# Two decoder layers on one core: activation tiles by ScalarE's DMA queue, two raw weight buffers, other token chunks, norm pieces and weight sums on VectorE

## The reference

```python
def rms_norm(x, g, eps=RMS_EPS):
    xf = x.astype(jnp.float32)
    y = xf * lax.rsqrt(jnp.mean(xf * xf, axis=-1, keepdims=True) + eps)
    return (y * g.astype(jnp.float32)).astype(x.dtype)

def swiglu(xn, w_gate, w_up, w_down):
    h = jax.nn.silu(jnp.einsum('bsd,df->bsf', xn, w_gate)) * jnp.einsum('bsd,df->bsf', xn, w_up)
    return jnp.einsum('bsf,fd->bsd', h, w_down)
...
        hp = hp + swiglu(rms_norm(hp, ln_ffn[layer]), w_gate[layer], w_up[layer], w_down[layer])
        hs = hs + swiglu(rms_norm(hs, ln_ffn[layer]), w_gate[layer], w_up[layer], w_down[layer])
```

## Time and profile before

| | us |
|---|---|
| median of three runs | 2750.6 |
| the profiled execution's own time | 2745.67 |
| its span, first to last instruction | 2743.8 |
| TensorE busy / VectorE / ScalarE / GpSimd | 2385.8 / 1658.9 / 972.0 / 850.5 |
| mean granted TensorE clock | 0.951 of full speed |

### The profile page before, as it was taken

The page is one execution under the profiler, slowest core; times in us unless marked ns, Lnnn a source line. Parts: engine busy times, 40 slices in busy tenths (PEclk is TensorE's granted clock), DMA queues, the critical chain, the costliest instruction groups (busy, mean ns, idle before and its releaser), DMA issues. The chain is left out here.

```text
span 2743.8 us, 47200 instructions
## 1 busy us (share of the span) xinstructions
PE 2385.8 (87%) x17889; PEld 2183.8 (80%) x17889; DVE 1658.9 (60%) x3570; ACT 972.0 (35%) x2144; POOL 850.5 (31%) x863
## 2 busy tenths in 40 slices
PE   8999998888899799999987887786999999878876
PEld 6788766555699699999987886786999899878876
DVE  4312166556755866767665665488767676656655
ACT  5211134455742433333332112454333333322123
POOL 0010100354321344343432225532343434322243
PEclk9999999999999899999998998898999999988988
DMA  4331499655620242434374443202433333744433
GB/s 155 106 108 44 156 388 405 221 168 168 207 69 16 97 161 104 157 108 147 118 297 172 153 161 106 77 21 97 155 110 141 124 128 136 283 187 153 153 115 108
DMA packets 178850, 410.13 MB, mean 149 GB/s; under 512 B 9683, under 2 KB 115492, under 8 KB 170187
## 3 DMA queue, kind: packets, MB, share of 16 engines
q1 hardware_dynamic: 172835, 359.70, 36.4%
q0 software_dynamic: 5808, 47.64, 5.0%
HBM read 302.52 MB, written 138.31 MB: 161 GB/s over the span
## 5 line engine op out<-in xcount | busy, mean ns | idle before, releaser
L2490 PE MATMUL ps<-xnr,wc 128*128 128x272 f32 x6336 | 854.3, 295 | 40.7 <-issue 15.6
L2490 PEld LDWEIGHTS ps<-xnr,wc 128*128 128x128 f32 x6336 | 835.6, 194 | 44.0 <-issue 42.0
L2490 PE MATMUL ps<-x2b,wc 128*128 128x272 f32 x2376 | 349.2, 302 | 141.9 <-DVE x L2059 97.1
L2490 PEld LDWEIGHTS ps<-x2b,wc 128*128 128x128 f32 x2376 | 324.9, 199 | 157.2 <-DVE x L2059 81.8
L2490 PE MATMUL ps<-x2a,wc 128*128 128x272 f32 x2376 | 335.8, 298 | 78.4 <-DVE ot L2003 45.8
L2490 PEld LDWEIGHTS ps<-x2a,wc 128*128 128x128 f32 x2376 | 319.4, 196 | 86.3 <-DVE wc L1958 48.4
L1302 POOL TENSOR_TENSOR wsum<-wr 128x512 f32<-128x512 f32 (+2 forms) x90 | 96.9, 1077 | 796.9 <-DMA wr<-w_down 389.0
L1958 DVE TENSOR_TENSOR wc<-wr,wc 128x512 fp32r<-128x512 f32 (+2 forms) x270 | 199.0, 737 | 213.4 <-ACT wc L1526 213.4
L1526 ACT ACTIVATE wc<-wr 128x512 fp32r<-128x512 f32 (+2 forms) x270 | 142.2, 527 | 406.9 <-DMA wr<-w_down 223.3
L2231 PE MATMUL ps<-wp,xn 128*128 128x512 f32 (+1 forms) x1080 | 245.4, 389 | 0.0
L2231 PEld LDWEIGHTS ps<-wp,xn 128*128 128x128 f32 (+1 forms) x1080 | 196.3, 182 | 48.9
(11 more groups left out here) (277 smaller groups left out, 3300.9 us busy)
## 6 DMA issues: line engine op xcount, KB each, us to landing
hidden<-stg SPq DMA_DIRECT2D x40, 1904.0 KB, 8.6
xnr<-hidden SPq DMA_DIRECT2D x40, 1088.0 KB, 10.3
wr<-w_up SPq DMA_DIRECT2D x22, 1024.0 KB, 10.2
wr<-w_gate SPq DMA_DIRECT2D x20, 1024.0 KB, 5.3
kraw<-cache_win_k_a SPq DMA_DIRECT2D x8, 2048.0 KB, 14.8
vraw<-cache_win_v_a SPq DMA_DIRECT2D x8, 2048.0 KB, 11.6
kraw<-cache_k_b SPq DMA_DIRECT2D x64, 256.0 KB, 5.8
vraw<-cache_v_b SPq DMA_DIRECT2D x64, 256.0 KB, 11.1
```

Source lines behind the costliest of these rows:

```text
L2490: r = mm(out, wc[:, q, a, kt * P:(kt + 1) * P], slot(moving_at(u, kt), q, b_), start=(q < 4 and kt == 0 and i == 0), stop=(kt == n - 1 and ...
```

## The change

- The hidden stores, the slot loads and the reload of x are issued by ScalarE, at places written into its stream, and no longer by SyncE. Slot loads of the second piece (n = 4 to 7) are moved to units 45 and 46.
- SyncE issues only the weights. The load of set w waits for the last set that used the same part of `wr` (`set_before`). `wr` grows from 2048 to 3072 columns: sets of depth 2 and 3 alternate between two places, sets of gate and up (depth 4) still have one. In layer 1 set 0 has a tile of its own, `wr0`. The copy of x to DRAM is issued ahead of set 1.
- The two sums in `wsum` for the sets of gate and up are made by VectorE, at the start of the unit before the set; GpSimd still makes the other two, and all four in the down pieces.
- The token chunks are 384, 288, 416 ahead of layer 0's FFN and 384, 256, 448 ahead of layer 1's (with 3, 2 and 4 row tiles).
- All norm differences go to VectorE, as single instructions over four tiles (128 x 1088), and so do the high and low parts of the normalised tiles. The quarters of tp 1 come later in unit 0, between its parts.
- The low parts of both hidden tiles of a block are made in the next block's first unit (gate tp 0), no longer half of them in the unit up tp 1. The stores follow in that unit's part 5 and the next unit's part 2.

```diff
-CH = ((0, 384), (384, 384), (768, 320))
+CH = {1: ((0, 384), (384, 288), (672, 416)), 3: ((0, 384), (384, 256), (640, 448))}
...
+        def set_place(w):
+
+            n = 512 * set_depth(w)
+            at_ = n * (w % 2) if n < 2048 else 0
+            return at_, at_ + n
+
+        def set_before(w):
+
+            a0, a1 = set_place(w)
+            return max(v for v in range(1, w) if set_place(v)[0] < a1 and a0 < set_place(v)[1])
...
                 if w == 1:
-                    sp.wait_ge(norm_pieces, 16 * norm_block(layer, 1) + 1)
+                    sp.wait_ge(norm_pieces, 16 * norm_block(layer, 1) + 16)
                 else:
-                    sp.wait_ge(set_lo, PARTS * set_number(layer, w))
+                    sp.wait_ge(set_lo, PARTS * (set_number(layer, set_before(w)) + 1))
...
             def ffn_sp(layer):
 
                 set_load(layer, 0)
-                set_load(layer, 1)
-                sp.wait_ge(norm_pieces, 16 * norm_block(layer, 1) + 16)
+                sp.wait_ge(group_added, ADD_PER * (layer + 1))
                 sp.dma_start(x_kept[:], x[:]).then_inc(x_stored, 16)
-                for u in range(UNIT_L):
-                    kind, b, _, tp = ffn_at(u)
-                    w = set_at(u)
-                    for n in range(SLOTS):
-                        if n not in KEPT and slot_free(n) == u - 1:
-                            slot_load(layer, n)
-                    if u == set_begin(w) and 1 <= w < SETS - 1:
-                        set_load(layer, w + 1)
-                    if 2 <= u - 1 < UNIT_A - 4 and ffn_at(u - 1)[0] == "up":
-                        hidden_store(layer, *ffn_at(u - 1)[1::2])
+                for w in range(1, SETS):
+                    if w == SETS - 2:
                         sp.wait_ge(part_done, done(layer, UNIT_Z + 3, PARTS - 1))
+                        sp.wait_ge(blocks_added, 24 * layer + 12)
...
+                    set_load(layer, w)
...
+            def transfers(layer, u, q):
+
+                b, r = divmod(u - 4, 4)
+                if 0 <= b < PAIRS - 1 and (r, q) in ((0, 5), (1, 2)):
+                    hidden_store(layer, b, r)
+                if (u, q) == (UNIT_A - 3, 6):
+                    x_load(layer, 0)
+                if (u, q) == (UNIT_A - 2, 2):
+                    x_load(layer, 1)
+
+            def slot_loads(layer, u):
+
+                for n in range(SLOTS):
+                    if n not in KEPT and u == (UNIT_A + 1 + n // 6 if 4 <= n < 8 else slot_free(n) + 1):
+                        slot_load(layer, n)
...
+                        if u == set_end(w) and w + 1 < UNIT_A // 2 and q == 0:
+                            set_sum(layer, w + 1)
                         if u == set_end(w) and w < SETS - 1 and q:
                             set_low(layer, w + 1, q - 1)
-                        if 0 < u <= UNIT_A and ffn_at(u - 1)[0] == "up" and q >= 3:
+                        if u in (UNIT_A - 1, UNIT_A) and q >= 3:
                             for i in ((0, 1), (2, 3), (4, 5), (6,))[q - 3]:
                                 hidden_low(layer, u - 1, i)
+                        elif 4 <= u < UNIT_A and u % 4 == 0:
+                            for i in ((0, 1, 2), (3, 4), (5, 6), (0, 1), (2, 3), (4, 5), (6,))[q]:
+                                hidden_low(layer, u - 2 if q < 3 else u - 1, i)
```

More of the change, by code:

```diff
@@ L562, in norm_block, with norm_at @@
             return 2 * layer + tp
+        NORM_PIECES = (((0, 0), (1, 0), (0, 1), (1, 1)), ((0, 0), (0, 1), (1, 1), (1, 0)))
+        NORM_SUMS = (V1, V2, V3, V4), (V1, V2, V4, V3)
+        NORM_HI = (V11, V21, V22, V2, V1, V3, V4), (V11, V2, V1, V3, V21, V22, V4)
+        NORM_LO = V11, V2, V1, V3, V21, V22, V4
+        def norm_at(order, n, tp, what):
+            return len(order[tp]) * n + order[tp].index(what) + 1
         def chunk_sum_bank(c):
@@ L1525, in set_high @@
                     act.wait_ge(set_sums, 4 * set_number(layer, w) + {2: 1, 1: 2, 3: 3, 5: 4}[q])
[L1526 removed]
+                act.activation(set_cols(w, wc[:, q, 0]), set_source(layer, w, q), ACT.Copy).then_inc(set_hi, 1)
             def norm_high(layer, tp, q):
                 n = norm_block(layer, tp)
[L1531 to L1539 removed]
+                place = {V11: (0, 0), V21: (1, 0), V22: (1, 1)}.get(q)
+                if place:
+                    act.wait_ge(norm_pieces, 4 * norm_at(NORM_PIECES, n, tp, place))
+                else:
+                    act.wait_ge(norm_sums, norm_at(NORM_SUMS, n, tp, q))
+                act.activation(normed(tp, q, 0), normed_plain(tp, q), ACT.Copy).then_inc(norm_hi, 1)
             def hidden_high(layer, u, q):
@@ L1943, in norm_low @@
             def norm_low(layer, tp, q):
                 n = norm_block(layer, tp)
-                place = (V11, V21, V22, V2, V1, V3, V4).index(q)
-                dve.wait_ge(norm_first, 8 * n + (8 if q in (V3, V22) else 4))
-                if q in (V2, V4):
-                    dve.wait_ge(norm_second, 8 * n + 8)
-                for kt in range(4):
-                    phys = kt + 4 * tp
-                    dve.wait_ge(norm_hi, 28 * n + 4 * place + kt + 1)
-                    tt(slot(phys, q, 1), slot_plain(phys, q), slot(phys, q, 0).bitcast(F32), ALU.subtract).then_inc(norm_lo, 1)
+                reader = {V11: V1, V2: V4, V1: V2, V3: V3, V21: V4, V22: V3, V4: V4}[q]
@@ new lines, in norm_low, with set_sum @@
+                dve.wait_ge(norm_sums, norm_at(NORM_SUMS, n, tp, reader))
+                dve.wait_ge(norm_hi, norm_at(NORM_HI, n, tp, q))
+                tt(normed(tp, q, 1), normed_plain(tp, q), normed(tp, q, 0).bitcast(F32), ALU.subtract).then_inc(norm_lo, 1)
+            def set_sum(layer, w):
+                n = set_number(layer, w)
+                dve.wait_ge(set_loaded[w % 2], set_loads(layer, w))
+                dve.wait_ge(set_lo, PARTS * n)
+                tt(set_cols(w, wsum[:, 0]), raw_quarter(layer, w, 0, 1), raw_quarter(layer, w, 1, 1), ALU.add).then_inc(set_sums, 1)
+                dve.wait_ge(set_sums, 4 * n + 1)
+                tt(set_cols(w, wsum[:, 1]), set_cols(w, wsum[:, 0]), raw_quarter(layer, w, 0, 0), ALU.subtract).then_inc(set_sums, 1)
@@ L2042, in down_out @@
                     if p:
-                        tt(kept, src, kept, ALU.add).then_inc(parts_dve, 1)
+                        tt(both, src, both, ALU.add).then_inc(parts_dve, 1)
                     return
@@ L2097, in ffn_dve @@
                     if u == 0:
-                        for v in (V1, V3, V21, V22, V4):
+                        norm_sum(layer, 1, V4)
+                        norm_low(layer, 1, V2)
+                        norm_low(layer, 1, V1)
+                        norm_sum(layer, 1, V3)
+                        for v in NORM_LO[3:]:
                             norm_low(layer, 1, v)
```

241 lines of the change are left out of this document (124 added, 117 removed).

## The result

The changed kernel takes 2514.3 us in the median of 4 runs (2510.5 to 2519.6), against 2750.4 for the kernel before (4 runs): ratio 0.914, 95% interval 0.912 to 0.916. The forecast was 2502, with 2465 to 2565 as its range. The profiled execution took 2515.3 us with a span of 2513.5, so 230.3 us of span are gone.

The account below looks back on a forecast made before the run. TensorE loses some 180 us per layer waiting on late weights or at lower clock afterwards. Savings 2 x (37 + 3.7 + 41.5 + 35 + 7) = 248.4 us give 2497.3 profiled, so 2502 forecast; range 2465 to 2565.

Parts of the forecast that it names:

- Gate and up: From unit 2: three stalls per block go, 37 us less per layer, 3.7 of 40.7 staying as slips; bounds 25 to 40.7.
- VectorE becomes the bound: Rival in gate and up: VectorE overloaded in up tp 1, load late again, 2.7 us per block, 2556 us; chance 0.13.
- Units 44 and 45: Weights no longer behind six slot loads, last hidden tile's order unchanged: 3.7 us less per layer, bounds -4 and 10.
- 4.62 and 1.8 less 1.8 and 1.5: Units 44 to 46: unit 45's stall and slow clock go; a ScalarE issue stall of 1.8 and slow clock of 1.5 come.
- Down pieces: From unit 46: weights load one set earlier, in a queue without slot loads; 41.5 us less per layer, bounds 30 and 44.
- the 3.3 us that I left: Down pieces: loss expected to remain of 44.8 us per layer, at the step from depth 2 to 3.
- its slot is freed too late in both kernels: Down pieces, step from depth 2 to 3: reason given, beside places one behind the other, for the 3.3 us left.
- The first rival: Down pieces: weights served in issue order behind slot loads, 4 us late plus 1.6 slow clock, six times; 2536 us; chance 0.10.
- the loop that I followed: Last piece: VectorE's last result through GpSimd's add, sums, high and low parts, back to last result; 8.6 us per period.
- The rival of 11.5 us: Last piece stays in its chain: GpSimd's adds between its sums, period 11.5 us, 2 x 20 less won, 2542; chance 0.12.
- Units 0 and 1: VectorE has fewer, larger instructions and less contention with GpSimd: 7 us less per layer, bounds -5 and 15.
- 2 us earlier: Units 0 and 1: VectorE's work from the reciprocal starts 2 us earlier, results of parts 1 and 2 going ahead of quarters.

Follow-up runs that it names:

- The kernel with x behind the weights: Against the changed kernel: SyncE reloads x behind the first two down sets, ScalarE's root behind norm pieces, last norm sum earlier; 2502.9 us, ratio 0.909.
- one place: Against the changed kernel: down weight sets back to one raw place, each load waiting for the copies of the set before; 2639.1 us profiled.
- lows spread: Against the changed kernel: hidden low parts back to seven behind each up unit instead of fourteen in gate tp 0; 2536.9 us profiled.

## Why the prediction was right, step by step

**Gate and up, 37 forecast, 38.3 and 39.5 measured.** The mechanism holds: the low parts moved, the load lands in 5.3, and the three stalls are gone. With the low parts spread again the second stall alone came back, and only with SyncE's queue and GpSimd's sums on top the old 483, which is the order of causes that the prediction gives. The forecast left 3.7 of the 40.7 as slips; some 2 are left. It priced the other two edits as harmless, and they are, but only behind the first. The rival "VectorE becomes the bound" did not come: 337.6 of 445 busy is 76%, less than the 81% forecast. VectorE's busy time grew by 6 to 9 us, not by 28. The run with the sums on GpSimd shows where the rest is: the sums add only 3 to 4 us net to VectorE, because its other instructions get shorter with GpSimd less busy.

**Units 44 and 45: the size right (3.7), the path wrong, so the agreement is luck.** The prediction's own terms, 4.62 and 1.8 less 1.8 and 1.5, make 3.1 and not 3.7. The 4.62 us went, and ScalarE's hold cost 0.34 and 0.23 in unit 46, not 1.8. In exchange the stall ahead of unit 44 grew from 5.9 to 8.85 us, in a place whose order I took for unchanged. The first down set was issued at 2211.80, 0.4 us after ScalarE had issued the last of 4.3 MB of x, and landed 13.9 us later (GpSimd and ScalarE at that time, then GpSimd again):

```profile
2225.73 0.74 POOL L1305 TENSOR_TENSOR wsum<-wr 128x256 f32<-128x256 f32 x1 [16.06 <-DMA wr<-w_down]
2225.74 0.42 ACT L1558 ACTIVATE wc<-wr 128x256 fp32r<-128x256 f32 x1 [3.48 <-DMA wr<-w_down]
...
2227.32 0.76 POOL L1313 TENSOR_TENSOR xnrf<-ot,xnrf 128x272 f32<-128x272 f32 x1
```

GpSimd makes the four differences of the last hidden tile (L1313 to L1319) only behind the sums of this set, so the late weights hold up the tile too. The kernel with x behind the weights shows it: 5.89 us again, 3 us per layer back; every run with x issued by SyncE, or later, has 5.89.

**Down pieces, 41.5 forecast, 36.6 and 36.2 measured.** The second place and the early load are most of the gain (one place gives 24 to 26 us back). The term that was too small is the 3.3 us that I left: 8.1 and 8.7 are lost. The step at unit 76 takes 3.8 and 4.5 of them inside unit 75 (in layer 1 the stalls of 0.84 and 3.24), the three piece ends, which I took for free, 3.2, and unit 46 some 0.7. The slow clock behind the step (7.04 us for 36 matmuls against 4.7 in layer 1) falls into the last piece. The reason "its slot is freed too late in both kernels" was wrong for the larger part: with set 38 loaded early the stall ahead of unit 76 stayed. It was 1.40 and 1.57 us before the change, and 1.33 and 1.30 with one place.

By the Trainium skill, "DMA: Bandwidth & Descriptors" ("Issuing engines are not separate DMA queues"), issuing from another engine brings only issue time. In the stage's time the pieces bear it out nearly: 166 by ScalarE's queue, 171 by SyncE's. The same page of the Trainium skill ("Queues, rings and completion order") has each DMA engine take turns between its queues. The landings at a piece's end agree: 6.5 and 9.4 us beside four slots in the other queue, 12.4 and 13.0 behind them in its own. Where the load was late anyway, in gate and up with spread low parts, that side shows in the time, 459 against 499, though there the order of the issues changed too. The first rival (weights share the slot loads' delay, 34 us) did not come.

**Last piece, 35 forecast, 36.8 and 36.2 measured.** A period is 8.9 in place of 8.6 without an output row, and 9.7, 10.4 and 9.0 with one, where 10 was forecast. TensorE waits 0.75 for VectorE in the first kind, which fits the loop that I followed; no run took the loop apart. The rival of 11.5 us was wrong.

**Units 0 and 1, 7 forecast, 1.8 and 0.5 measured: this step failed.** Counted from the first matmul of unit 0 it is 0.1 and 0.9. From the reciprocal to the last low part VectorE took 26.5 us in place of 29.9 (25 and 30 forecast). What failed was the start, "2 us earlier": the reciprocal begins 13.4 us after the first matmul, and 13.2 before the change. ScalarE's root of the next chunk stands ahead of a norm piece, and VectorE waits for it (ScalarE, then VectorE):

```profile
893.25 0.61 ACT L1645 ACTIVATE crstd<-ps,small 128x416 f32<-128x416 f32 x1 [5.30 <-PE ps L2345]
893.76 1.10 ACT L1568 ACTIVATE xnr<-xnrf 128x1088 fp32r<-128x1088 f32 x1
```

```profile
894.96 1.29 DVE L1985 TENSOR_TENSOR xnr<-xnrf,xnr 128x1088 fp32r<-128x1088 f32 x1 [2.18 <-ACT xnr L1568]
...
928.59 0.69 DVE L1992 TENSOR_TENSOR wsum<-wr 128x512 f32<-128x512 f32 x1
```

The last row is the other part: the two sums (1.4 us), which I had counted for gate and up, stand here too, ahead of unit 1's first result. TensorE's wait of 11.17 us did shrink, to 5.43, but one of 1.43 in unit 1 grew to 3.54. TensorE is also busy for 3 us more with the same matmuls (32.4 us in place of 29.2), at a granted clock of 0.76 in place of 0.77. Moving the root and one norm sum gave 3.4 in layer 0 and 1.1 to 2.7 in layer 1, the 2.7 with the old chunks and a slightly higher clock (0.78, against 0.76). Four quarters did fall to 1.73 us with GpSimd quiet, so the contention of the earlier trace rows is gone.

**Chunks: 0 forecast, and no more than the clock's own scatter measured.**

## What to carry to other kernels

A wait for a load in a written order is cured first by freeing its place early: a second place for the down weights (0.5 to 0.75 MB) was worth some 60 us per layer, and moving seven small instructions to another unit of the engine that frees the place made the queue and the sums indifferent, each undone by itself. When several edits serve one stall, undo them singly and together, since their gains don't add. Before giving an engine DMAs to issue, look at which weights stand behind or beside its largest transfer, and at what the engine itself has to do next.

## What the runs showed of the hardware that was not expected

- A load of 1 MB in SyncE's queue landed in 5.8 us in the median with a 1.9 MB store issued 1.5 us later by ScalarE (lows spread), and in 10.2 us with a store 0.6 us ahead of it in its own queue and one 5.1 us behind it. But 0.5 MB of down weights, issued 0.4 us after the last of 4.3 MB of x in ScalarE's queue, took 13.9 us, and 3.9 with x behind them: another queue does not always protect a load.
- A DMA issue held ScalarE 0.33 us (store), 0.53 (a slot's second half), and 8.17 us with x and three halves of slots just ahead of it. In the changed kernel the last half of four slots held it 1.88 to 4.83 us at each of the six piece ends, in a unit in which it had nothing else to do, and TensorE had no stall over 0.2 us behind it.
- The pool phase of the same kernel took 86.6 or 93.9 us at a granted clock of 0.90 or 0.81, so a single profile can't tell 7 us there.
